# Cross attention's products with the values: from two full-precision records each to three passes over rounded halves

## What is computed

```python
s = jnp.einsum('blhd,bmhd->bhlm', q, k).astype(jnp.float32) * (XATTN_HEAD_DIM ** -0.5)
p = jax.nn.softmax(s, axis=-1).astype(v.dtype)
o = jnp.einsum('bhlm,bmhd->blhd', p, v).reshape(B, L, D_MODEL)
return o @ wo
```

## Time and profile before

| | |
|---|---|
| median of three runs | 1717.59 us |
| the profiled execution's own time | 1715.55 us |
| its span in the trace | 1713.8 us |
| PE busy | 1684.9 us (98%) |
| DVE busy | 869.6 us (51%) |
| POOL busy | 818.7 us (48%) |
| ACT busy | 643.0 us (38%) |
| mean granted clock of PE | 0.998 |

### The profile page before, as it was taken

One profiled execution on the slowest core, in us unless ns is written; L12 is line 12 of the kernel. 1 busy time (PEld: TensorE's weight loads), 2 busy tenths in 40 slices (PEclk: granted clock), 3 DMA queues, 4 the chain that ended last, 5 costly groups with the idle time before them and its releaser, 6 DMA issues.

```text
span 1713.8 us, 21271 instructions
## 1 busy us (share of the span) xinstructions
PE 1684.9 (98%) x7500; PEld 1366.5 (80%) x7500; DVE 869.6 (51%) x1166; ACT 643.0 (38%) x827; POOL 818.7 (48%) x604
## 2 busy tenths in 40 slices
PE   8999999999999999999999999999999999999997
PEld 5687777878878888888888888888888888888886
DVE  6688787565346524243557676753333432232234
ACT  6534333534234111121255656563333432222222
POOL 3446145634325544444445666564444444444443
PEclk9999999999999999999999999999999999999999
DMA  5122112333212222222222333332222222222222
GB/s 211 61 74 86 50 50 87 111 111 113 72 49 99 98 89 95 98 98 92 92 98 99 118 103 111 110 103 94 97 98 98 90 95 97 98 98 98 98 96 101
DMA packets 47631, 164.41 MB, mean 96 GB/s; under 512 B 5141, under 2 KB 7317, under 8 KB 47322
## 3 DMA queue, kind: packets, MB, share of 16 engines
q1 hardware_dynamic: 44864, 158.51, 26.7%
q10 hardware_dynamic: 2714, 5.17, 0.8%
HBM read 161.57 MB, written 2.10 MB: 95 GB/s over the span
## 4 chain that ended last, share of the span: by engine, by line
PE 48%; issue 21%; POOL 14%; DVE 2%; POOLq 0%; DMA 0%; ACT 0%; DVEq 0%; SPq 0%
PE ps L629 16%; PE ps L630 16%; PE ps L631 16%; POOL m_w_lo L549 13%; POOL m_QL L590 0%; DVE m_h L2531 0%; DVE m_cbuf L1985 0%; DMA m_raw<-in_strips 0%; DVE m_cbuf L1983 0%; PE ps L836 0%; DVE m_cbuf L1977 0%; DVE ps L2117 0%; DVE m_s L2108 0%; DVE ps L2110 0%; DVE m_qs L2125 0%
## 5 line engine op out<-in xcount | busy, mean ns | idle before, releaser
L549 POOL TENSOR_TENSOR m_w_lo<-m_raw,m_w_hi 128x512 fp32r<-128x512 f32 x582 | 787.0, 1374 | 841.2 <-ACT m_w_hi L1238 840.8
L1238 ACT ACTIVATE m_w_hi<-m_raw 128x1024 fp32r<-128x1024 f32 x291 | 307.0, 1057 | 612.5 <-DMA m_raw<-in_strips 612.3
L629 PE MATMUL ps<-m_XH,m_w_hi 128*128 128x512 f32 x1096 | 436.8, 399 | 2.7 <-POOL m_w_lo L549 2.1
L631 PE MATMUL ps<-m_XH,m_w_lo 128*128 128x512 f32 x1096 | 427.1, 390 | 0.0
L630 PE MATMUL ps<-m_XL,m_w_hi 128*128 128x512 f32 x1000 | 389.5, 389 | 0.0
L629 PEld LDWEIGHTS ps<-m_XH,m_w_hi 128*128 128x128 f32 x1096 | 205.9, 188 | 53.6 <-issue 6.7
L631 PEld LDWEIGHTS ps<-m_XH,m_w_lo 128*128 128x128 f32 x1096 | 205.8, 188 | 43.4
L630 PEld LDWEIGHTS ps<-m_XL,m_w_hi 128*128 128x128 f32 x1000 | 187.8, 188 | 39.8 <-issue 1.7
L629 PE MATMUL ps<-m_FH,m_w_hi 128*128 128x512 f32 (+1 forms) x438 | 169.3, 387 | 0.2 <-DVE m_FL L1759 0.2
L630 PE MATMUL ps<-m_FL,m_w_hi 128*128 128x512 f32 (+1 forms) x438 | 169.1, 386 | 0.0
L631 PE MATMUL ps<-m_FH,m_w_lo 128*128 128x512 f32 (+1 forms) x438 | 169.1, 386 | 0.0
(11 more groups left out here) (404 smaller groups left out, 2201.5 us busy)
## 6 DMA issues: line engine op xcount, KB each, us to landing
m_raw<-in_strips SPq DMA_DIRECT2D x294, 512.0 KB, 3.2
m_x_in<-in_x SPq DMA_DIRECT2D x4, 512.0 KB, 8.6
m_x_res<-in_x ACTq DMA_DIRECT2D x1, 2048.0 KB, 9.2
m_memf<-in_mem SPq DMA_DIRECT2D x1, 1024.0 KB, 16.1
m_decay<-in_decay ACTq DMA_DIRECT2D x1, 1024.0 KB, 10.3
out<-m_h SPq DMA_DIRECT2D x8, 128.0 KB, 1.8
out<-m_h ACTq DMA_DIRECT2D x8, 128.0 KB, 1.8
m_w<-in_w ACTq DMA_DIRECT2D x1, 512.0 KB, 7.9
```

Of the source, the lines that this page charges most:

```text
L549: nc.gpsimd.tensor_tensor(w_lo[:, c], raw[:, c], f(w_hi[:, c]), ALU.subtract).then_inc(lo_ready, 1)
L629: pe.matmul(dst, hi[:, c], xh, start=first, stop=False)
L631: return pe.matmul(dst, lo[:, c], xh, start=False, stop=last)
L1238: act.activation(w_hi[:, c], raw[:, c], ACT.Copy).then_inc(hi_ready, 1)
```

## The change

V gets a high half VH (rounded by ACT) and a low half VL (V minus VH, by POOL, written over V). PT is declared float32r, so ACT's copy rounds it; a new DVE step `turned_low` subtracts it from the transposed probabilities in PSUM and gives PTL. `attended` calls `three_of` with these instead of one full-precision matmul. New semaphores: `v_high`, `v_low`, `pt_low`. The waits of `turned` and `attended` on ACT's copy become waits on `pt_low`. POOL's `lows` is cut in two around the new work.

```diff
-        PT = at("PT", 4 * T, 120 * KB)
+        PT = at("PT", 4 * T, 120 * KB, F32R)
+        PTL = at("PTL", 4 * T, 32 * KB, F32R)
+        VH = at("VH", 2 * D, 40 * KB, F32R)
+        VL = at("VL", 2 * D, 152 * KB + 128, F32R)
...
@@ POOL
-            lows(S_HY + 18, N_STRIPS)
+            lows(S_HY + 18, S_WQ + 2)
+            for mt in range(2):
+                pool.wait_ge(v_high, mt + 1)
+                c = slice(mt * D, (mt + 1) * D)
+                nc.gpsimd.tensor_tensor(VL[:, c], V[:, c], f(VH[:, c]), ALU.subtract).then_inc(v_low, 1)
+            lows(S_WQ + 2, N_STRIPS)
@@ PE, turned(hd)
                 if hd >= 1:
-                    pe.wait_ge(s_tcopy, hd)
+                    pe.wait_ge(pt_low, hd)
@@ PE, attended(hd)
-                pe.wait_ge(s_tcopy, hd + 1)
+                pe.wait_ge(pt_low, hd + 1)
                 if hd >= 1:
                     pe.wait_ge(o_pair, 2 * hd)
+                else:
+                    pe.wait_ge(v_low, 2)
                 for dt in range(2):
                     for mt in range(2):
-                        c = mt * D + (2 * hd + dt) * P
-                        mm = pe.matmul(ps[:, 4 + dt, :], V[:, c:c + P], tile(PT, hd % 2 * 2 + mt),
-                                       start=(mt == 0), stop=(mt == 1))
+                        mm = three_of(ps[:, 4 + dt, :], VH, VL, mt * KT + 2 * hd + dt, tile(PT, hd % 2 * 2 + mt),
+                                      tile(PTL, hd % 2 * 2 + mt), mt == 0, mt == 1)
                     mm.then_inc(s_o, 1)
@@ ACT
             for u in range(3):
                 ahead(S_WQ + u)
+                if u == 1:
+                    act.wait_ge(mixed, 8)
+                    act.wait_ge(kv_out, KT + 4)
+                    for mt in range(2):
+                        c = slice(mt * D, (mt + 1) * D)
+                        act.activation(VH[:, c], V[:, c], ACT.Copy).then_inc(v_high, 1)
             exps(0)
@@ DVE
+            def turned_low(hd):
+
+                dve.wait_ge(s_tcopy, hd + 1)
+                if hd >= 2:
+                    dve.wait_ge(s_o, 2 * (hd - 1))
+                c = slice(hd % 2 * 2 * T, (hd % 2 * 2 + 2) * T)
+                dve.tensor_tensor(PTL[:, c], ps[:, 2:4, :].rearrange("p a b -> p (a b)"), f(PT[:, c]), ALU.subtract
+                                  ).then_inc(pt_low, 1)
...
             maxima(1)
+            turned_low(0)
             query_out(5)
             normalised(1)
             outputs_pair(0)
             query_out(6)
             maxima(2)
+            turned_low(1)
             query_out(7)
             normalised(2)
             outputs_pair(1)
             maxima(3)
+            turned_low(2)
             normalised(3)
             outputs_pair(2)
+            turned_low(3)
             outputs_pair(3)
```

More of the change, by code:

```diff
@@ L412, in build @@
         s_tcopy = sem("s_tcopy")
+        pt_low = sem("pt_low")
+        v_high = sem("v_high")
+        v_low = sem("v_low")
         s_o = sem("s_o")
```

## The result

| | before | after |
|---|---|---|
| median | 1717.59 us | 1726.35 us |
| the profiled execution's own time | 1715.55 us | 1726.18 us |
| span in the trace | 1713.8 us | 1724.4 us |
| ratio to before | | 1.0054, 95% interval 1.0044 to 1.0065 |

The changed kernel is slower by 0.54%: 1717.59 x 0.0054 = 9.3 us, between 7.6 and 11.2 by the interval. The forecast was 1727.6 in a range of 1724.0 to 1730.4.

The account below looks back on a forecast made before the run. PE, busy 98% of the time, was taken to bound the kernel. Stall 9.9 plus clock 2.7 minus gain 2.6 gave +10.0 us on the median 1717.59, so 1727.6 us, range 1724.0 to 1730.4.

Parts of the forecast that it names:

- The gain: PE's 16 products with the values: three passes of 0.232 us replace two records of 0.429, saving 2.6 us.
- count of four passes: Alternative estimate for those products: full precision counted as four array passes, three for four saving 3.7 us; not used in sum.
- The stall: PE before query strip 2 waits for POOL's low part, held behind ACT's copy and two VL subtractions: 9.9 us.
- The clock: PE's clock falls during the idle before query(2); 13 to 14 passes at the lower clock cost 2.7 us.
- the first rival: The clock holds or comes back at once after the stall: +7.3 us, 1724.9 us; chance 0.12.
- ACT's copies: Two copies of V on ACT fill 2.0 of 2.30 us spent waiting for a transfer: costed at nothing.
- VL in time for its products: POOL finishes VL at 433.9, and the products with it come 25 us later: costed at nothing.
- POOL's later strips: Strips S_WQ + 3 to + 5 last until 443.9; the first is ready at 438.9, before query(3): free.
- DVE: Four added PSUM subtractions, at most 1.38 us each, fit before the products with the values: nothing, upper end 0.5 us.
- The second: Everything new is late: slower POOL +0.9, DVE 0.5, longer cold stretch +1.3; +12.7 us, 1730.3; chance 0.08.
- The third: Query strip 2 isn't held up if ACT's first copy signals by 419.1: 1715.0 us; chance 0.03.
- The fourth: The three passes of the products with the values take 0.429 us each: +19.5 us, 1737.1; chance 0.01.

Follow-up runs that it names:

- e1: Changed kernel with POOL's list cut two strips later, before S_WQ + 4 instead of S_WQ + 2: 1714.88 us, ratio to before 0.9988.
- e2: Changed kernel, POOL's cut left alone, with ACT's two copies of V moved in front of the root of the norm: 1714.07 us, ratio 0.9984.
- e8: Kernel before, with its full-precision products with the values done five times over: 1772.80 us, ratio 1.0326.
- e4: Kernel before, full-precision products kept, plus only ACT's copies and POOL's subtractions at the change's places, VL read by nobody: 1729.65 us, ratio 1.0070.
- e5: Changed kernel with POOL waiting for ACT's first copy, then doing strip S_WQ + 2 before both VL subtractions: 1722.74 us, ratio 1.0028.
- e6: Changed kernel with one VL subtraction ahead of strip S_WQ + 2 and the other behind it: 1725.06 us, ratio 1.0043.
- e3: Changed kernel with POOL's list cut one strip later, before S_WQ + 3: 1717.27 us, ratio to before 1.0000.
- e9: e1 with the three-pass products with the values done five times over: 1757.62 us, ratio 1.0241.
- e7: e1 with DVE's subtraction done twice per head: 1716.53 us, ratio 1.0001.

## Why the prediction was right

**The gain.** 2.6 us forecast, 2.64 in the trace, and e1 and e2 leave 0.12 and 0.16% below before. The estimate of 3.7 us by a count of four passes is not borne out: e8 shows two records of 0.429 us again.

**The stall.** Forecast 9.9 with 9.6 as its lower bound, found 9.43, a little below the bound. The chain was as written: root, two aheads, first copy, two subtractions, one pair of low parts. The small difference is in the starts, which overlap more than I added up (4.65 us for the VL pair instead of 4.80, 0.1 or so at each handover).

**The clock.** Forecast 2.7 us, found 1.58. This is the term that was mis-sized: "I take the fall and the price of the start". The fall was right, the price was that of one other execution. With the same idle it was 1.58, 1.69, 1.90 and 2.91 us, so one execution's figure could not give the term. The start of the run would have said so if read more than once: in the thirteen profiles the passes shown with about 0.63 us there number from 6 to 13, and the trace that the prediction read has 12. By the trace the sum is 8.4 instead of 10.0 us: 1.1 of the difference is this term, 0.5 the stall. The Trainium skill, "TensorE: Matmul & The Clock Gate", section What's actually happening, has the half rate as the default state and says that the point of the change varies from run to run. The six profiles here with 4.66 us of idle or more agree with both: the clock fell in each, and with 9.26 us of idle the cost varied by 1.3 us.

**What was luck.** That the clock falls was the right choice, but the evidence was thinner than it looked. The prediction took from the earlier trace rows that 1.79 us of idle leave the clock at 1.00. That held there and in seven others. Behind the same wait of 1.79 to 1.82 us, in code that is the same, it fell in five of the thirteen profiles (e2, e4, e5, e6, e8); e2's PE timeline and its busy time by stretch:

```profile
372.53 0.50 PE L640 MATMUL ps<-m_XH,m_w_hi 128*128 128x512 f32 x1 [1.79 <-POOL m_w_lo L555]
373.11 0.63 PE L642 MATMUL ps<-m_XH,m_w_lo 128*128 128x512 f32 x1
...
376.51 0.39 PE L641 MATMUL ps<-m_XL,m_w_hi 128*128 128x512 f32 x1
```

```profile
374.00:376.00 2.00, 2.00 (x6) 1.61 (x5) 0.00 (x0) 0.00 (x0) 2.00 (x3) 0.50 1.03 394
```

From that wait's end to the norm's product are 49.9 to 50.0 us in these five, and 48.5 to 48.6 in seven of the others (49.0 in e3, with no slow pass): a fall cost 1.4 us. So the earlier trace rows could not tell for or against the first rival, and such falls are a part of the spread between executions of one kernel.

**What was costed at nothing.** ACT's copies: right, e1. VL in time for its products: right, with 34 us to spare (434.90 to 469.11) where the text had 25. POOL's later strips: right, eight low parts end at 444.78 and query(3) begins at about 448. DVE: right in its result, and closer than the text had it in one place. The subtraction took 1.22 us, not 1.38, but normalised(3) behind it took 2.91 us instead of the 1.15 of before, because it starts later and so into POOL's pair of low parts (499.20 to 501.78); the last section has the evidence. It ended at 502.46, and turned(3) started at 502.71: 0.25 us of room where I had 1.7. DVE's timeline, to be held against the earlier trace rows:

```profile
498.21 1.22 DVE L2284 TENSOR_TENSOR m_PTL<-ps,m_PT 128x1024 fp32r<-128x1024 f32 x1 [2.91 <-ACT m_PT L1644]
499.35 0.17 DVE L2291 RECIPROCAL m_misc<-m_misc 128x4 f32<-128x4 f32 x1
499.55 2.91 DVE L2296 TENSOR_SCALAR m_PR<-m_PR,m_misc 128x256 f32<-128x256 f32 x4
```

**Rivals.** The first (the clock holds) fell in all six profiles with 4.66 us of idle or more. The second (all late) did not come as a whole; its third part alone, a longer cold stretch, shows in e4 with 2.91 us. The third named 419.1 as the turning point; e2 put the signal ahead of it and the loss was gone. The fourth fell with e9.

## What to carry to other kernels

An engine's list is a queue: an item that waits holds everything behind it, ready or not. Before putting one in, write down when its input is signalled and when the item behind it is due; here that sum (one late copy, two subtractions, one strip) gave the loss before anything ran. The same work two places later in the list turned +0.54% into -0.12%, and moving its input forward did as well (-0.16%): what counts is when the item in front can be finished, that is the time of its signal and then its own work. Of the 9.26 us of idle 4.66 were the late signal and 2 x 2.30 the two subtractions (e5, e6).

## What the runs showed of the hardware that was not expected

- An idle of 4.66 us cost as much clock as one of 9.26: the granted clock was still 1.00 when PE came back and fell 0.6 us later, and 1.64 us were lost (443.13 - 435.90 - 5.59) against 1.58 to 2.91; 6.96 us of idle cost 2.47. In the changed kernel the clock had fallen inside the idle: 430:432 reads 0.61, and PE's last pass before it starts at 427.73.
- An idle of 1.8 us cost nothing in eight profiles and was followed by a fall in five, again after PE was back at work (e2: back at 372.53, passes 0.43 us apart from 373.11 to 376.10). The length of an idle alone does not say whether the clock falls. An idle of 0.33 us (e3) was not followed by one. What lies between 1.8 and 4.66 us was not tried in this stretch.
- DVE's four 128x256 scalings of a head's probabilities take as long as POOL's low parts (SBUF to SBUF) stand beside them. With no POOL work beside them they took 1.14 to 1.15 us (the last head in before, e4 and e8); with 0.33 us of it 1.26 (e7); with 0.62 to 0.69 us of it beside them 1.56 to 1.64 (the other three heads of before among them), with 0.91 us 1.84 (e7, below), with 1.29 us 2.23 (e1), and with 2.23 us 2.91 (the changed kernel, e1, e2, e3, e6 and e9). DVE's subtraction, which reads PSUM, took 1.22 us with POOL beside it all the way (e7) and 1.21 without. POOL's own pair took 2.50 us with no scalings beside it and 2.58 to 2.60 with them: the slowdown falls on DVE. No run moved POOL's work alone, so this is read from what stood beside what.

```profile
490.39 1.84 DVE L2298 TENSOR_SCALAR m_PR<-m_PR,m_misc 128x256 f32<-128x256 f32 x4
```
